# Conformer and short-conv trunk on eight cores: input projections two output chunks at a time by Strassen's scheme, x streamed through a small buffer, one output-projection round per layer

## The reference, cut to what matters

```
def hybrid_layer(x, ...):                      # D_MODEL 1024, x (B, T, 1024)
    h = rmsnorm(x, norm_g)
    p = h @ w_in                               # 1024 -> 7 * 1024
    a_val, a_gate, z_a, gb, gc, hb, z_b = split(p)
    u = a_val * sigmoid(a_gate)
    ca = causal_dwconv(u, width 31)            # per channel
    ca = head_layernorm(ca + conv_a_b) * g + b
    y_a = silu(ca) * silu(z_a)
    v = gc * hb
    y_b = gb * causal_dwconv(v, width 3) * silu(z_b)
    return x + concat(y_a, y_b) @ w_out        # 2048 -> 1024
# two layers, then a last rmsnorm; the last rows of u and v are outputs too
```

## Time and profile before

| | |
|---|---|
| runs | 1106.86, 1107.42, 1330.08 us; median 1107.42 |
| profiled execution | span 1103.3 us on the slowest core (core 5), 1101.4 on the fastest; its time outside the span is not given |
| busy | TensorE 1087.8, VectorE 760.8, ScalarE 452.9, GpSimd 285.1 us |
| instructions | 21027 |

### The profile page before, as it was taken

How to read it: one execution, slowest core, us unless ns; L and a number is a source line. 1 busy time by engine, 2 the same in 40 slices (tenths; PEclk the granted TensorE clock), 3 DMA queues, 4 the chain that set the end, 5 groups by cost and what they waited for, 6 DMA issues and landing times.

```text
span 1103.3 us, 21027 instructions; the slowest of 8 cores (1101.4 to 1103.3 us)
## 1 busy us (share of the span) xinstructions
PE 1087.8 (99%) x7008; PEld 538.8 (49%) x7008; DVE 760.8 (69%) x1608; ACT 452.9 (41%) x725; POOL 285.1 (26%) x454
## 2 busy tenths in 40 slices
PE   6999999999999999999999999999999999999998
PEld 3445455455454544444444545445545454454545
DVE  3695776887768684864774587587867858567456
ACT  5862343243530443354342244332543224424555
POOL 7552121031120210113471112112121102111165
PEclk9999999999999999999999999999999999999999
DMA  9947569476764552681034756864764734535325
GB/s 232 231 96 143 74 122 179 72 111 99 125 117 82 88 89 48 87 144 30 1 46 80 138 90 116 166 119 75 116 94 104 123 66 78 87 60 90 87 89 227
DMA packets 178457, 116.48 MB, mean 106 GB/s; under 512 B 139184, under 2 KB 151344, under 8 KB 178288
## 3 DMA queue, kind: packets, MB, share of 16 engines
q0 software_dynamic: 34352, 54.97, 31.6%
q1 hardware_dynamic: 143568, 59.62, 24.2%
q10 hardware_dynamic: 432, 0.55, 0.1%
HBM read 131.78 MB, written 35.14 MB: 151 GB/s over the span
## 4 chain that ended last, share of the span: by engine, by line
PE 96%; DMA 2%; POOL 1%; ACT 0%; issue 0%; DVE 0%; ACTq 0%; DVEq 0%; POOLq 0%
PE psb L647 92%; DMA x_sb<-x_d 2%; PE psb L882 2%; PE psb L883 2%; PE psb L1093 1%; PE psb L1096 0%; POOL toep L1169 0%; POOL x_sb L1132 0%; POOL wsl L614 0%; ACT tmp L707 0%; DVE toep L860 0%; ACT big L772 0%; ACT big L1115 0%; DVE big L1106 0%; POOL u_sb L1138 0%
## 5 line engine op out<-in xcount | busy, mean ns | idle before, releaser
L647 PE MATMUL psb<-h_sb,wsl 128*128 128x512 bf16 (+1 forms) x4160 | 758.0, 342 | 0.7 <-DVE h_sb L762 0.4
L647 PEld LDWEIGHTS psb<-h_sb,wsl 128*128 128x128 bf16 x4160 | 346.8, 98 | 377.7 <-issue 3.9
L647 PE MATMUL psb<-y_sb,wsl 128*128 128x512 bf16 (+2 forms) x960 | 182.0, 338 | 0.2 <-DVE x_sb L1032 0.2
L1032 DVE TENSOR_TENSOR x_sb<-x_sb,psb 128x512 f32<-128x512 f32 (+2 forms) x240 | 131.5, 582 | 46.4 <-PE psb L647 45.6
L614 POOL DMA_DIRECT2D wsl<-w_in_r x104 | 56.1, 548 | 341.5 <-PE psb L647 217.9
L647 PEld LDWEIGHTS psb<-y_sb,wsl 128*128 128x128 bf16 x960 | 82.1, 98 | 86.2 <-issue 0.3
L1013 DVE SCALAR_TENSOR_TENSOR tmp<-vbuf,cw_b_sb,tmp 128x512 f32<-128x512 bf16 (+1 forms) x160 | 102.8, 654 | 23.0 <-ACT tmp L1010 12.2
L980 DVE TENSOR_TENSOR vbuf<-psb,tmp 128x512 bf16<-128x512 f32 (+1 forms) x80 | 47.5, 595 | 65.4 <-PE psb L647 64.0
L815 DVE SCALAR_TENSOR_TENSOR u_sb<-tmp,psb 128x512 bf16<-128x512 f32 (+1 forms) x96 | 49.6, 518 | 61.0 <-PE psb L647 56.5
L1018 ACT ACTIVATE tmp<-psb 128x512 f32<-128x512 f32 (+1 forms) x80 | 41.2, 521 | 112.6 <-PE psb L647 69.0
L806 ACT ACTIVATE tmp<-psb 128x512 f32<-128x512 f32 (+1 forms) x76 | 38.9, 518 | 117.4 <-PE psb L647 106.7
(11 more groups left out here) (106 smaller groups left out, 992.1 us busy)
## 6 DMA issues: line engine op xcount, KB each, us to landing
wsl<-w_in_r POOLq DMA_DIRECT2D x104, 256.0 KB, 6.6
scr_u<-u_sb SPq DMA_DIRECT2D x16, 704.0 KB, 7.1
up_sb<-scr_u SPq DMA_DIRECT2D x16, 704.0 KB, 7.4
scr_c<-big SPq DMA_DIRECT2D x16, 640.0 KB, 6.3
big<-scr_c SPq DMA_DIRECT2D x16, 640.0 KB, 4.8
wt_sb<-wt_d POOLq DMA_DIRECT2D x64, 128.0 KB, 3.5
x_sb<-x_d POOLq DMA_DIRECT2D x12, 512.0 KB, 20.3
wsl<-w_out_r POOLq DMA_DIRECT2D x24, 256.0 KB, 5.0
```

What stands on the lines that cost most here:

```text
L647: ins = e.matmul(bank(v, n), lhsT=l_(), rhs=r_(), start=(first and i == 0), stop=(last and i == len(pairs) - 1))
L1032: dve((lambda e: e.tensor_tensor(out=xs(m, part), in0=xs(m, part), in1=bank(v, n), op=ALU.add)), n, [v, xr], [xr], name=f"x{q}.{m}")
```

## The change

**Pairs.** The two chunks of P2 to P7, a1 to a7 and b0 to b7 are computed together, for two blocks of 512 columns at a time (q0 with q1, q2 with q3). Weights and h are each cut in two along k (four slices each), which makes a 2 x 2 by 2 x 2 block product. It is done with seven half-depth products (four matmuls each) in place of eight, by Winograd's form of Strassen's scheme. Its operand sums of h (`t_forms`, L903) are made once per layer on VectorE, in bf16, in three slots of 2048 columns for each pair of blocks; one of them replaces the first half of h in q1 and q3. The sums of the weights (`sums`, L921) are four GpSimd adds for each pair of chunks. The seven products are put together in PSUM and by VectorE: ScalarE copies -P1 into a bank (`sd`, L948), P6 is added to it by TensorE, then P7, then P4; P5 is copied to SBUF (`p5`, L948); `c12` (L961) and `c22` (L971) are VectorE subtractions. The banks that ScalarE seeds are 6 and 7 alone (`CLEAN`), so two are open at a time. q4 is projected as before. Step Z keeps its number of matmuls, with one more weight sum for q1 and q3 (L1132).

**x streamed, one round.** `x_sb` is gone. x of layer 0 lies in the space of `y_sb` and of the new `xst` (six slots of 1024 f32 columns) during the first phase; later it is read again from DRAM block by block at the output projection, and layer 0 writes the new x to `x_mid` in DRAM. `y_sb` has 13 chunks in place of five, all 16 chunks of a layer go into one output round (`out_final`), and its 16 weight chunks lie in whatever is free then (`HOMES`). `wsl` has 7 slots.

**Moved.** The Toeplitz copies go from VectorE to ScalarE (L1019). In step b the taps are multiplied with the SiLU on GpSimd (L1243), and VectorE has one product left (L1249). `ORDER`, the keys (`BG`), `SLACK` and the costs of the scheduler are new; PSUM's eight banks are shared out as 5 for projections, 1 for z, 2 for convolutions and statistics.

```diff
-    "C0 b0 Z0 P2 a1 b1 C1 P3 C2 Z1 P4 P5 O4 C3 a2 Z2 C4 b2 a3 P6 Z3 b3 C5 P7 Z4 O4 a4 C6 Z5 b4 a5 b5 a6 C7 b6 a7 b7u0 Z6u1 Z7up",
+    "C0 b0 C1 a1 Z0 P2 b1 Z1 C2 P3 a2 P4 C3 b2 Z2 P5 a3 C4 b3 Z3 Z4 P6 C5 a4 C6 P7 C7 b4 a5 b5 Z5 a6 b6 a7 Z6u0 b7u1 Z7up",
+    "C0 b0 C1 a1 Z0 P2 b1 P3 C2 P4 a2 Z1 b2 C3 P5 Z2 C4 a3 P6 b3 Z3 Z4 C5 a4 b4 a5 C6 Z5 P7 C7 b5 a6 b6 a7 Z6u0 Z7u1 b7up",
+CLEAN = (6, 7)
+STEPSP = "P10 P50 P60 P11 P20 P51 P61 P30 P21 P70 P40 P31 P71 P41 s"
+STEPSa = "P10 P11 P50 P60 P51 P20 P30 P61 P21 P70 P40 P31 P71 s P41"
+STEPSb = "P10 P50 P60 P11 P51 P20 P61 P30 P21 P31 P71 P70 s P40 P41"
+HOMES = [[("toep", 2, 2), ("big", 2, 2), ("sum", 2, 2), ("w", 2, 1), ("h", 2, 1)],
+         [("toep", 2, 2), ("w", 6, 1), ("sum", 2, 2), ("big", 1, 2)]]
+CAPS = {"proj": 5, "conv": 2, "z": 1}
+TMPS = {"tmp": 4, "snap": 2, "zp": 2, "tap": 1}
-SLACK, SLACK_DMA, SLACK_FIRST, QUIET = 1.5, 3.5, 2.0, 40.0
+SLACK, SLACK_DMA, SLACK_FIRST, QUIET = 0.5, 3.5, 2.0, 40.0
-    NY, NW, NBIG, NTMP = 5, 9, 3, 6
-    x_sb = sb("x_sb", [128, KC * T], F32)
+    NY, NW, NBIG, NX, NSUM = 13, 7, 3, 6, 2
+    xst = sb("xst", [128, NX, 1024], F32)
+    wsum = sb("wsum", [128, NSUM, 2048], BF16)
+    zsum = sb("zsum", [128, 1, 512], BF16)
-        "bank": Pool(8, {"proj": 6, "conv": 2, "stat": 2}, keep=1),
-        "w": Pool(NW, spare=None),
+        "bank": Pool(8, CAPS, spare=None, clean=CLEAN),
+        "w": Pool(NW, spare=None),
...
+    def t_forms(after=()):
+        for p in range(2):
+            q1, q2 = 2 * p, 2 * p + 1
+            t = tf[p] = [V("xs") for _ in range(3)]
+            tap = (lambda i, t=t: xsth[:, t[i].slot, :])
+            def tt(out, a, b, op, rd, wr, i):
+                dve((lambda e: e.tensor_tensor(out=out(), in0=a(), in1=b(), op=op)), 2048, rd, wr, rate=2, lock=True, after=after, name=f"T{i}.{p}")
+            b11, b21 = (lambda q1=q1: half(q1, 0)), (lambda q1=q1: half(q1, 1))
+            b12, b22 = (lambda q2=q2: half(q2, 0)), (lambda q2=q2: half(q2, 1))
+            t1, t2, t4 = (lambda tap=tap: tap(0)), (lambda tap=tap: tap(1)), (lambda tap=tap: tap(2))
+            tt(t1, b11, b12, ALU.subtract, hr4(q1, 0) + hr4(q2, 0), [t[0]], 1)
+            tt(t2, b22, t1, ALU.add, hr4(q2, 1) + [t[0]], [t[1]], 2)
+            tt(t4, b21, t2, ALU.subtract, hr4(q1, 1) + [t[1]], [t[2]], 4)
+            tt(b12, b12, b22, ALU.subtract, hr4(q2, 1), hr4(q2, 0), 3)
+    def sums(w1, w2):
+        s = V("sum")
+        parts = rs(4)
+        ap = (lambda i: wsum[:, s.slot, 512 * i:512 * i + 512])
+        def add(i, a, b, rd):
+            S.op("pool", (lambda e: e.tensor_tensor(out=ap(i), in0=a(), in1=b(), op=ALU.add)), 0.95, rd, [parts[i]], lock=True, holds=[s], name=f"S{i}")
+        add(0, (lambda: wh(w2, 0)), (lambda: wh(w2, 1)), [w2])
+        add(1, (lambda: ap(0)), (lambda: wh(w1, 0)), [parts[0], w1])
+        add(3, (lambda: ap(1)), (lambda: wh(w1, 1)), [parts[1], w1])
+        add(2, (lambda: wh(w2, 0)), (lambda: wh(w1, 0)), [w1, w2])
+        return s, parts
+    def pair(w1, w2, f1, f2, nm, **kw):
+        s, sr = sums(w1, w2)
+        hold = kw.pop("holds", [])
+        ws = lambda i, k: wsum[:, s.slot, 512 * i + 128 * k:512 * i + 128 * k + 128]
+        g = []
+        for p in range(2):
+            g.append(dict(p=p, q=(2 * p, 2 * p + 1), b=V("bank", "proj"), e=V("bank", "proj"), a=V("bank", "seed", "seed"),
+                          c=V("snap"), t=tf[p]))
+        def prod(v, lhs, rhs, rd, first, held, name):
+            def fn(e):
+                for k in range(4):
+                    ins = e.matmul(bank(v, 512), lhsT=lhs(k), rhs=rhs(k), start=first and k == 0, stop=True if not first else k == 3,
+                                   skip_group_check=not first)
+                return ins
+            S.op("pe", fn, c_pe([512] * 4), rd, [v], holds=hold + held, name=name, **kw)
+        wk = lambda w, i: (lambda k: wsl[:, w.slot, 512 * i + 128 * k:512 * i + 128 * k + 128])
+        hk = lambda q, i: (lambda k: half(q, i)[:, 512 * k:512 * k + 512])
+        tk = lambda t, i: (lambda k: xsth[:, t[i].slot, 512 * k:512 * k + 512])
+        sk = lambda i: (lambda k: ws(i, k))
+        cp = lambda o, i, rd, wr, scale, name: act((lambda e: e.activation(out=o(), in_=i(), func=AF.Copy, scale=scale)), 512, rd, wr, tab=None, name=name)
+        def step(what, i):
+            d = g[i]
+            q1, q2 = d["q"]
+            if what == "P1":
+                prod(d["b"], wk(w1, 0), hk(q1, 0), [w1] + hr4(q1, 0), True, [], f"P1{nm}.{i}")
+                cp((lambda: bank(d["a"], 512)), (lambda: bank(d["b"], 512)), [d["b"]], [d["a"]], -1.0, f"sd{nm}.{i}")
+            elif what == "P5":
+                prod(d["e"], sk(0), tk(d["t"], 0), [sr[0], d["t"][0]], True, [s], f"P5{nm}.{i}")
+                cp((lambda: tm(d["c"], 512)), (lambda: bank(d["e"], 512)), [d["e"]], [d["c"]], 1.0, f"p5{nm}.{i}")
+            elif what == "P6":
+                prod(d["a"], sk(1), tk(d["t"], 1), [sr[1], d["t"][1]], False, [s], f"P6{nm}.{i}")
+                dve((lambda e: e.tensor_tensor(out=bank(d["e"], 512), in0=tm(d["c"], 512), in1=bank(d["a"], 512), op=ALU.subtract)),
+                    512, [d["c"], d["a"]], [d["e"]], name=f"c12{nm}.{i}")
+            elif what == "P2":
+                prod(d["b"], wk(w1, 1), hk(q1, 1), [w1] + hr4(q1, 1), False, [], f"P2{nm}.{i}")
+                f1(q1, d["b"])
+            elif what == "P3":
+                prod(d["e"], sk(3), hk(q2, 1), [sr[3]] + hr4(q2, 1), False, [s], f"P3{nm}.{i}")
+                f1(q2, d["e"])
+            elif what == "P7":
+                prod(d["a"], sk(2), hk(q2, 0), [sr[2]] + hr4(q2, 0), False, [s], f"P7{nm}.{i}")
+                dve((lambda e: e.tensor_tensor(out=tm(d["c"], 512), in0=bank(d["a"], 512), in1=tm(d["c"], 512), op=ALU.subtract)),
+                    512, [d["a"], d["c"]], [d["c"]], name=f"c22{nm}.{i}")
+                f2(q2, d["c"])
+            else:
+                prod(d["a"], wk(w2, 1), tk(d["t"], 2), [w2, d["t"][2]], False, [], f"P4{nm}.{i}")
+                f2(q1, d["a"])
+        for tok in {"P": STEPSP, "a": STEPSa, "b": STEPSb}[nm[0]].split():
+            if tok[0] == "s":
+                f1(4, proj(w1, 4, name=f"{nm}.4", holds=hold, **kw))
+                f2(4, proj(w2, 4, name=f"{nm}.4", holds=hold, **kw))
+            else:
+                step(tok[:2], int(tok[2]))
...
-                wg, wv = w_pair(tok, (w_in_r[l, 8 + j], w_in_r[l, j]))
-                for q in range(NB):
-                    p1_block(l, j, q, wg, wv)
-                p1_end(l, j)
+    def p1(l, j):
+        wg, wv = w_load(w_in_r[l, 8 + j]), w_load(w_in_r[l, j])
+        if WINO:
+            ths = {}
+            def f1(q, v):
+                ths[q] = p1_gate(j, q, v)
+            pair(wg, wv, f1, lambda q, v: p1_val(j, q, v, ths[q]), f"P{j}")
...
+            if c < TACT:
+                act((lambda e, p=p, c=c: e.activation(out=toep[p, tp.slot, :].rearrange("p (m x) -> p m x", x=128)[:, :, 32 * c:32 * c + 32],
+                                                      in_=wt_sb[p, w.slot, :].rearrange("p (m a) -> p m a", a=32), func=AF.Copy)),
+                    512, [w], [tp], sbuf=True, tab=None, name=f"tp{j}.{qt}")
+                continue
...
+    def proj_t(w, zs, q, **kw):
+        v = V("bank", "z", "full")
+        pairs = [((lambda k=k: w_ap(w, k)), (lambda k=k: hv(k, q))) for k in range(4)] + \
+            [((lambda k=k: zsum[:, zs.slot, 128 * k:128 * k + 128]), (lambda k=k: hv(4 + k, q))) for k in range(4)]
+        mm("proj", v, 512, pairs, [w, zs] + [h_r[k][q] for k in range(KC)], **kw)
+        return v
...
+        def f1g(q, v):
+            f1_(q, v)
+            n = BLOCKS[q][1]
+            sz, a = szs[q], taps(q)
+            S.op("pool", (lambda e: e.tensor_tensor(out=tm(sz, n), in0=tm(a, n), in1=tm(sz, n), op=ALU.mult)), 0.15 + n * 0.0021, [a, sz], [sz],
+                 lock=True, name=f"gz{j}.{q}")
...
+        def f2g(q, v):
+            n = BLOCKS[q][1]
+            sz = szs[q]
+            dve((lambda e: e.tensor_tensor(out=y.ap(q), in0=sv(v, n), in1=tm(sz, n), op=ALU.mult)),
+                n, [v, sz], [y.res[q]], after=y.after, name=f"yb{j}.{q}", **y.kw())
...
-    def out_round(l, chunks, ys):
-        ws = [w_load(w_out_r[l, c]) for c in chunks]
-        for q in range(NB):
-            for m in range(KC):
-                out_block((q, 0, BLOCKS[q][1]), m, [w_lhs(w) for w in ws], ws, ys)
+    def x_stage(l, q):
+        x = xcur[q] = X(q)
+        src = x_d if l == 0 else x_mid
+        c0, n = BLOCKS[q]
+        w = 2 * n if q < 4 else KC * n
+        for i, v in enumerate(x.vs):
...
+        xr = x.r(m, part)
+        dve((lambda e: e.tensor_tensor(out=x.s(m, part), in0=x.s(m, part), in1=bank(v, n), op=ALU.add)),
+            n, [v, xr], [xr], holds=x.hold(m), name=f"x{q}.{m}")
+        if l == 0 and (m % 2 == 1 if q < 4 else m == KC - 1):
+            x_store(q, m // 2 if q < 4 else 0)
```

507 lines of the change are left out of this document (323 added, 184 removed).

## The result

The change makes the kernel slower: 1178.39 us (median of 6 runs) against 1106.94 in the same session, a ratio of 1.0635, 95% interval 1.0617 to 1.0653. The forecast was 1050 us, faster, with a range that ended at 1086. In some executions four of the eight cores show a lower granted clock and take longer, on the chip of e1 to e9 cores 4 to 7 in nearly all, so the ratios leave such executions out and the experiments are told by cores 0 to 3.

The account below looks back on a forecast made before the run. TensorE was taken to bound the kernel, busy 439.78 of 440 us in the middle. Span 1103.3 - 72.1 + 10 + 4.8 = 1046 us, plus 4.1 outside the span, gave 1050 us; range 1036 to 1086.

Parts of the forecast that it names:

- Matmuls removed, -72.1: Pairs: 336 fewer matmuls of 512 columns at 0.2157 us, less 0.4 for two short ones, wholly on the path.
- +10: Middle: waits at more hand-overs with VectorE at 82%, a fifth of the upper end, in us.
- +4.8: First pair of layer 0: TensorE waits for up_sb before the first convolution, 17.3 us less 12.5 of cover.
- All three stay under TensorE, so their sum costs nothing: Whole kernel: VectorE 65%, ScalarE 68%, GpSimd 56% busy, so their added work costs no time by itself.
- upper bound of 48: Middle: TensorE waits out one whole GpSimd add per pair, 42 x 1.15 = 48 us.
- port: Rival: VectorE and GpSimd block each other in the middle, weight sums come late, 48 + 5, 1088 us; chance 0.11.
- 44 of 47 us: Middle, one j: VectorE's two-SBUF-input operations, 19.9 us, and GpSimd's work, 24.2 us, added as one queue.
- 2 us if late: Output rounds: the 16 weight chunks need slots of the last pair; put at nothing, 2 us if late.
- 11 us against 6.6 us to landing: Layer 1's output weights: some 11 us before first use cover two or three issues and 6.6 us to landing.
- x late: Rival: x loads late at eight changes of block in the output rounds, 24 us and 2 more, 1076 us; chance 0.08.
- The head, at 0: Start of the kernel: unchanged, since x arrives as before; no cost.
- Banks: Rival: seven links through two seeded banks set the pace; 1143 us at 1.35 us per hand-over; chance 0.06.

Follow-up runs that it names:

- e1: Changed kernel with the pairs alone taken back, the moved copies and product and streamed x kept: 1158.0 us, +52 against the kernel before.
- e9: Changed kernel with the two matmuls that seed the banks moved behind the first phase: 1171.3 us against the changed kernel's 1172.3.
- e5: Changed kernel with the 184 sums of weights on VectorE in bf16, not on GpSimd: 1140.7 us, +35 against the kernel before.
- e15: e6 with four GpSimd subtractions per pair that nobody waits for: +127 us against the kernel before, ratio 1.1114, with e6 at +14.3 beside it.
- e12: Changed kernel without pairs, with late state copy and b0's weights loaded early: +23 us against the kernel before, ratio 1.0208.
- e10: e6 with b0's two weight chunks loaded during the first phase into a slot of y_sb: +5.5 us against the kernel before, ratio 1.0057.
- e14: e10 in a searched order of steps, products and priorities: 1092.72 us against 1109.59 for the kernel before, ratio 0.9848.
- e6: Changed kernel with weight sums on VectorE and the state copy and last-stage constants later: +12.6 and +14.3 us against the kernel before, ratio 1.0113.

## Why the prediction was wrong

**Matmuls removed, -72.1: right.** 1080.7 to 1008.7 us of matmul work at the pitch of the earlier trace rows.

Core 3's span missed the forecast one (1046) by 120 us: 59 in the middle (69 against the +10), 20 between 60 and 200 us (25 against the +4.8), 33 at the end and 8 in the head, where I had put nothing.

**"All three stay under TensorE, so their sum costs nothing", and "+10" for the middle: this step failed.** 69 us were lost between 200 and 900 us, above even the upper bound of 48. Two errors lie in it. First the durations. I took the taps at 0.748, LayerNorm's products at 1.49 and GpSimd's sum at 1.154 from the earlier trace rows, a trace in which GpSimd was busy for 26%; they measured 0.965, up to 2.12 (L1084) and 1.41 in the middle (100 to 500 us, core 3). VectorE's sum came to 787 and not 679, GpSimd's to 623 and not 583; ScalarE's, which has no part in it, to 700 against 712. Secondly the rule: I scaled from a VectorE that cost nothing at 73%, in a kernel where TensorE hung on it in no short chain. Half a pair is a chain of seven links between TensorE, ScalarE and VectorE, and then one blocked operation is a wait of TensorE's: `c12` alone accounts for 19.7 us in twelve waits on core 7, though it never took longer than 0.70 itself; it started late. The two longest of the twelve have different causes. One is the port (next paragraph). The longest, 7.9 us, is not. GpSimd's queue stood still for 8.8 us ahead of a weight load, until output weights had landed; the copies into `vbuf` stand behind that load, the tap waited for them, and `c12` stands behind the tap. GpSimd, then VectorE, then TensorE:

```profile
466.85 0.53 POOL L705 DMA_DIRECT2D wsl<-w_in_r  x1 [8.79 <-DMA big<-w_out_r]
...
468.02 1.61 DVE L1227 SCALAR_TENSOR_TENSOR tmp<-vbuf,cw_b_sb,tmp 128x512 f32<-128x512 bf16 x2 [9.92 <-POOL vbuf L1187]
469.54 0.69 DVE L961 TENSOR_TENSOR psb<-tmp,psb 128x512 f32<-128x512 f32 x1
...
470.38 1.87 PE L940 MATMUL psb<-h_sb,wsum 128*128 128x512 bf16 x4 [7.90 <-DVE psb L961]
```

**The rival "port" had a mechanism that the runs show, at a chance of 0.11.** A stretch of the changed kernel (core 7) shows it better than the earlier trace rows did. VectorE, then GpSimd:

```profile
159.00 1.64 DVE L1227 SCALAR_TENSOR_TENSOR tmp<-vbuf,cw_b_sb,tmp 128x512 f32<-128x512 bf16 x1
160.56 0.68 DVE L961 TENSOR_TENSOR psb<-tmp,psb 128x512 f32<-128x512 f32 x1
161.16 1.84 DVE L1073 TENSOR_TENSOR big<-big,mean_sb 128x2560 bf16<-128x2560 bf16 x1
162.93 1.65 DVE L1227 SCALAR_TENSOR_TENSOR tmp<-vbuf,cw_b_sb,tmp 128x512 f32<-128x512 bf16 x1
```

```profile
157.83 2.26 POOL L921 TENSOR_TENSOR wsum<-wsl 128x512 bf16<-128x512 bf16 x2 [0.53 <-DMA wsl<-w_in_r]
160.05 3.97 POOL L921 TENSOR_TENSOR wsum<-wsum,wsl 128x512 bf16<-128x512 bf16 x2
```

GpSimd's second sum ends at 157.83 + 2.26 = 160.09; the tap, begun at 159.00, ends 0.55 us behind that. The next two sums take 3.97 us in place of 2.3 and the taps 1.64 and 1.65 in place of 0.75, one ending behind the other each time. I priced this by adding up the two engines' work for one j, 44 of 47 us, and called it "not over 100%". A queue that is 94% full was no cover here. The whole way to TensorE is seen once, at the longest tap of all. It was recorded as begun 0.15 us ahead of five sums in a row and ended 0.56 us behind the last of them, after 6.28 us; `c12` and TensorE came next. VectorE, GpSimd, TensorE:

```profile
824.26 6.28 DVE L1227 SCALAR_TENSOR_TENSOR tmp<-vbuf,cw_b_sb,tmp 128x512 f32<-128x512 bf16 x1 [0.80 <-ACT tmp L1224]
830.47 0.68 DVE L961 TENSOR_TENSOR psb<-tmp,psb 128x512 f32<-128x512 f32 x1
...
824.41 2.27 POOL L921 TENSOR_TENSOR wsum<-wsl 128x512 bf16<-128x512 bf16 x2
...
828.84 1.14 POOL L921 TENSOR_TENSOR wsum<-wsum,wsl 128x512 bf16<-128x512 bf16 x1
...
831.29 1.01 PE L940 MATMUL psb<-h_sb,wsum 128*128 128x512 bf16 x2 [3.46 <-DVE psb L961]
```

How large the port's part is stays open. Moving the sums to VectorE gave 32 us back (e5), which is below the 48 of the rival's price but has VectorE make the sums, and eases GpSimd's queue as well; the rest of the 128 us between 1050 and 1178 lies in the other terms of this section. e5 and e15 show that GpSimd's load is the cause of the part that they move, and not the lateness of the sums; neither separates the port from GpSimd's queue as such, on which weight loads, `vbuf`'s copies and the product stand too. TensorE's longest list entry in e15 is VectorE:

```profile
PE psb L717 <- DVE big L1069: 27.0, 11, 5.2
```

The Trainium skill, "SBUF — State Buffer", section "SBUF: two separate sides", says that a VectorE operation with two SBUF inputs and a GpSimd operation that reads SBUF exclude each other for their whole length. The trace agrees now for two-input operations too (1.64 us for 0.75); those with an input in PSUM, which that rule leaves out, kept their 0.69 throughout.

**The first pair, +4.8: right in part, size wrong.** Two waits came where the working had them (on core 7 0.8 us for `sd` at 77.7 and 2.6 for the first sums at 81.3), with 2.8 more for ScalarE's Toeplitz copies at 99.5 and some 3 of low clock, but the loss from 60 to 200 us is 25. The wait for `up_sb`, which was to set the start of the first convolution at 89.8 us, never came: on core 7 TensorE went to the convolution straight from the pair, at 95.43. The working stopped at the first convolution. Behind it GpSimd, which holds its weight loads back while `up_sb` is read, issued the next five only at 93.2 us (core 3); before, free slots of y had held early weights, and the streamed x now lies in them. I costed b0's chunks alone. The two mended kernels bear this out for the part without pairs, where 21 of 22 us go (e12); with pairs 11 of 25 do (e10), and of the other 14 the searched order took 3 (e14), and what holds the rest stays open.

**The end of layer 1, "2 us if late": wrong.** 33 us behind 900, of which 14 are there without pairs (e1). "11 us against 6.6 us to landing" took the landing of a lone chunk. Here eleven output weights (2.8 MB), 2.8 MB of x, the constants (0.6) and the copy (1.7) come within 50 us, and the DMA engines' share is about 1 from 1000 to 1030 us (core 7). The rival "x late" had looked at x alone; that x's own loads delayed the weights is likely and wasn't tried.

**The head, at 0: 8 us.** Part is low clock (1.7), part an order in which six matmuls of the norm's sums stand ahead of weights' matmuls and wait 2.3 us for ScalarE's squares. e9 ruled out the seeding matmuls. The rest was not tried and stays open.

**The clock.** It had no term. 17 us on core 3 of the changed kernel (23 on core 7), and it follows the waits: 13 in e1, 3 in e12, 4 in e14, 42 in e15.

**"Banks"** can't be ruled out as a part. e5 was to tell it from the port by a fuller VectorE, but VectorE's busy time fell there, so it doesn't test this rival. By itself the chain of links through two seeded banks does not make a loss of 69 us, since the same chain in e6 goes with 29 us in the middle; but 6 of these are there without pairs, TensorE waits for ScalarE's copy `sd` for 9.8 us in twelve waits (e6, core 3), and another order brings the middle to 23.5 us (e14). I had put +10 on the hand-overs; by these numbers some 17 to 23 us come with the pairs even where the sums are VectorE's.

## What to carry to other kernels

Before giving GpSimd elementwise work beside VectorE, add up only VectorE's operations with both inputs in SBUF and GpSimd's together as one queue, and ask that it be far from full; a bf16 sum of 512 columns took VectorE 0.49 us where it took GpSimd 1.15 to 1.41, so the "free" engine was the dearer. A duration read from a trace in which the neighbour was mostly idle was here a lower bound. And follow a busy engine's queue in order: what is behind a load that waits, waits too. When a buffer is freed or reused, list what had been parked in it early (here weights), and look at every transfer that starts in the same 20 us as the one that you count on.

## What was not expected of the hardware

One busy GpSimd can cost TensorE over 100 us: 168 subtractions of 1.2 us, 203 us of an engine that has more than half its time free, made the kernel 113 us longer (e15), in an order planned without them. Behind a wait of 17.5 us the granted clock was 0.50, and even shorter idle times in short succession were followed by a stretch of 3.4 us at 0.50 (core 3, after 24 us in the head; 0.9, 0.4 and 2.3 us idle ahead of it); at that level a matmul of 512 columns takes twice its 0.2157 us.
